# Expert stage of a two-layer inference step: a sixth place for weights, loads in the order in which places come free, and two blocks in the loop

## What is computed

```python
g_idx = jnp.argmax(g_logits, axis=-1)                 # one of 4 groups
top_v, top_i = lax.top_k(e_sel, TOP_K_IN_GROUP)       # 2 of its 8 experts
...
for g in range(N_GROUPS):
    a = jnp.einsum('td,edf->tef', x, w_gate[g])       # 1024 -> 256
    u = jnp.einsum('td,edf->tef', x, w_up[g])
    hid = jax.nn.silu(a) * u * comb[:, g, :, None]
    y = y + jnp.einsum('tef,efd->td', hid, w_down[g]) # 256 -> 1024
```

## Time and profile before

| What | us |
|---|---|
| median of 3 runs (1677.84 to 1684.67) | 1681.57 |
| profiled execution, its own time | 1689.48 |
| its span, first to last instruction | 1687.8 |
| PE busy | 1295.8 (77%) |
| DVE busy | 642.0 (38%) |
| ACT busy | 429.5 (25%) |
| POOL busy | 253.2 (15%) |

### The profile page before, as it was taken

How to read it: one execution, slowest core, us unless ns; L and a number is a source line. 1 busy time by engine, 2 the same in 40 slices (tenths; PEclk the granted TensorE clock), 3 DMA queues, 4 the chain that set the end, 5 groups by cost and what they waited for, 6 DMA issues and landing times. The chain is left out here.

```text
span 1687.8 us, 24274 instructions
## 1 busy us (share of the span) xinstructions
PE 1295.8 (77%) x8176; PEld 904.7 (54%) x8176; DVE 642.0 (38%) x1579; ACT 429.5 (25%) x971; POOL 253.2 (15%) x376
## 2 busy tenths in 40 slices
PE   6888899988838888777178898899797397787650
PEld 4777778867635444333145676667586253444320
DVE  4555544335452222212632343344463422222118
ACT  3555544443011101001111243344510111100010
POOL 0111122210111121221310000000011112211214
PEclk9988889998958988988588999999898599888775
DMA  4212224305077999983710000000031899999733
GB/s 152 65 58 65 78 90 151 107 15 197 38 305 266 394 395 385 393 285 125 277 42 16 14 28 14 14 13 14 30 125 41 328 370 392 377 386 359 278 102 108
DMA packets 59634, 290.91 MB, mean 172 GB/s; under 512 B 12209, under 2 KB 22641, under 8 KB 42497
## 3 DMA queue, kind: packets, MB, share of 16 engines
q1 hardware_dynamic: 49280, 270.62, 42.8%
q0 software_dynamic: 10240, 18.90, 3.7%
HBM read 274.86 MB, written 29.29 MB: 180 GB/s over the span
## 5 line engine op out<-in xcount | busy, mean ns | idle before, releaser
L1741 PE MATMUL psum<-w_gu,moe_experts_xgT 128*64 128x256 f32 x2048 | 264.1, 403 | 25.1 <-DVE moe_experts_xgT L1804 21.3
L1741 PEld LDWEIGHTS psum<-w_gu,moe_experts_xgT 128*64 128x64 f32 x2048 | 152.7, 147 | 138.5 <-issue 84.3
L1789 ACT ACTIVATE moe_experts_yo<-psum 64x512 f32<-64x512 f32 x64 | 37.8, 590 | 396.5 <-DMA y_d<-moe_experts_yo,moe_slots 333.4
L1816 DVE COPY moe_experts_yo<-psum 64x512 f32<-64x512 f32 x64 | 44.3, 693 | 242.1 <-DMA y_d<-moe_experts_yo,moe_slots 200.2
L1757 PE MATMUL psum<-w_dn,moe_experts_hidT 128*64 128x512 f32 x416 | 126.0, 736 | 9.6 <-issue 9.6
L194 PE MATMUL psum<-x_hi,ab_w_hi 128*128 128x288 f32 x384 | 126.7, 330 | 4.3 <-DVE ab_k_tok L852 3.2
L1731 PE MATMUL psum<-ident,mix 64*128 64x64 f32 x512 | 48.6, 241 | 98.4 <-DMA mix<-x_d,moe_tokens 98.3
L195 PE MATMUL psum<-x_lo,ab_w_hi 128*128 128x288 f32 x384 | 116.8, 304 | 0.0
L196 PE MATMUL psum<-x_hi,ab_w_lo 128*128 128x288 f32 x384 | 116.7, 304 | 0.0
L1804 DVE COPY moe_experts_xgT<-psum 128x512 f32<-128x512 f32 x64 | 44.3, 692 | 177.1 <-PE psum L1731 177.0
L1731 PEld LDWEIGHTS psum<-ident,mix 64*128 64x128 f32 x512 | 40.4, 151 | 126.4 <-issue 126.4
(11 more groups left out here) (289 smaller groups left out, 2297.8 us busy)
## 6 DMA issues: line engine op xcount, KB each, us to landing
w_gu<-in_w_gate_up SPq DMA_DIRECT2D x64, 2048.0 KB, 20.4
w_dn<-in_w_down SPq DMA_DIRECT2D x52, 1024.0 KB, 14.8
xT<-in_w_down SPq DMA_DIRECT2D x12, 1024.0 KB, 15.6
w_gu<-in_w_out SPq DMA_DIRECT2D x4, 2048.0 KB, 17.1
w_gu<-y_d SPq DMA_DIRECT2D x16, 512.0 KB, 7.1
xT<-cum_d SPq DMA_DIRECT2D x8, 544.0 KB, 7.2
w_q<-in_w_ab SPq DMA_DIRECT2D x8, 512.0 KB, 7.4
w_k<-in_w_ab SPq DMA_DIRECT2D x8, 512.0 KB, 8.2
```

The costliest lines, as they stand in the source:

```text
L1741: last = nc.tensor.matmul(gu(s)[h * CB:(h + 1) * CB, 0:EH], xgT[:, s % 2, j, :], w_gu[n][:, j, h * EH:(h + 1) * EH], start=(j == 0), stop= ...
L1816: nc.vector.tensor_copy(yo[s % 2][:, BANK:D], y(s)[CB:P, :]).then_inc(y_dve, 1)
```

## The change

- `DEEP` is 6. The down tiles of places 4 and 5 and a quarter of the gate/up tile of place 5 lie in `xT`; that gate/up tile is loaded by two DMAs (12 KB and 4 KB per partition). Six experts are loaded ahead of the expert stage.
- SP issues gate/up of b+1 ahead of down of b, in the order up(b+1-6), down(b-6) in which PE is done with them.
- The loop has `TRIP` = 2 blocks (30 and 31 here); 0 to 29 are written out. Each written-out run and each trip is now a chain of its own: PE and DVE end the last block's work ahead of the next chain's first block.
- POOL alternates gather and scatter in the loop.
- g and b are loaded at the end of SP's list, into place 2, and no longer have tiles of their own.
- In place of common counters each place has its own count of uses; `copy_x` and `copy_h` lose a second wait.

```diff
-DEEP = 5
-FIRST = NE - RING
+DEEP = 6
+TRIP = 2
+FIRST = NE - TRIP
@@ route, SyncE
-                prefetch_down(k, sp, layer, [0, 1])
                 for n in range(2, DEEP):
+                    prefetch_down(k, sp, layer, [n - 2])
                     prefetch_gate_up(k, sp, layer, [n])
-                    prefetch_down(k, sp, layer, [n])
+                prefetch_down(k, sp, layer, [DEEP - 2, DEEP - 1])
@@ experts
-            for b in range(FIRST):
-                step(b, b % RING, 0, b + 1 < FIRST)
+            def chain(blocks):
+                first(*blocks[0])
+                for n, block in enumerate(blocks):
+                    step(block, blocks[n - 1] if n else None, blocks[n + 1] if n + 1 < len(blocks) else None)
+                last(*blocks[-1])
+            chain([(b, b % TRIP, 0) for b in range(FIRST)])
             with eng.Fori(0, n_trips) as i:
-                first_of_trip(RING * i + FIRST, 0, i)
-                for s in range(RING):
-                    step(RING * i + FIRST + s, s, i, s + 1 < RING)
-            last(RING * n_trips + FIRST - 1, RING - 1)
+                chain([(TRIP * i + FIRST + s, s, i) for s in range(TRIP)])
@@ experts, SyncE
-                sp.dma_start(r["g"][:], k.ln_g[layer, 1:2, :].to_broadcast([P, D])).then_inc(r["g_in"], 16)
-                sp.dma_start(r["b"][:], k.ln_b[layer, 1:2, :].to_broadcast([P, D])).then_inc(r["g_in"], 16)
                 for b in range(DEEP, FIRST):
                     n = b % DEEP
-                    sp.wait_ge(gu_ready, b - DEEP + 1)
-                    load_gate_up(k, sp, layer, b, gu_in[n], w_gu[n])
-                    sp.wait_ge(y_ready, b - DEEP + 1)
-                    load_down(k, sp, layer, b, dn_in[n], w_dn[n])
+                    sp.wait_ge(gu_used[n], b // DEEP)
+                    load_gate_up(k, sp, layer, b, gu_in[n], k.w_gu[n])
+                    if b > DEEP:
+                        n = (b - 1) % DEEP
+                        sp.wait_ge(dn_used[n], (b - 1) // DEEP)
+                        load_down(k, sp, layer, b - 1, dn_in[n], w_dn[n])
...
+                sp.wait_ge(gu_used[2], len(range(2, FIRST, DEEP)))
+                sp.dma_start(r["g"], k.ln_g[layer, 1:2, :].to_broadcast([P, D])).then_inc(r["g_in"], 16)
+                sp.dma_start(r["b"], k.ln_b[layer, 1:2, :].to_broadcast([P, D])).then_inc(r["g_in"], 16)
@@ experts, GpSimd
                 with pool.Fori(0, n_trips) as i:
-                    for s in range(RING):
-                        gather(RING * i + FIRST + s, s, RING * i + s + 1)
-                    for s in range(RING):
-                        scatter(RING * i + FIRST - RING + s, s, RING * i + s + 1)
+                    for s in range(TRIP):
+                        gather(TRIP * i + FIRST + s, s, i, TRIP * i + s + 1)
+                        scatter(TRIP * i + FIRST - RING + s, s, TRIP * i + s + 1)
@@ experts, VectorE
-                    hold(dve, passed, (x_turned, b + 1), *since(gu_ready, b - 1))
+                    hold(dve, passed, done(x_used, b, s, trip, RING))
@@ mixer_out_and_mixture
-        k.w_dn = [c.enter_context(k.nc.sbuf_tensor(f"w_dn{n}_{layer}", [P, JE, D], F32))[:, :, :] for n in range(DEEP - 1)]
+        k.w_gu.append([c.enter_context(k.nc.sbuf_tensor(f"w_gu{DEEP - 1}_{layer}", [P, J - 2, 2 * EH], F32))[:, :, :],
+                       room[:, 2 * JE * D:2 * JE * D + 4 * EH].rearrange("p (j n) -> p j n", j=2)])
+        k.w_dn = [c.enter_context(k.nc.sbuf_tensor(f"w_dn{n}_{layer}", [P, JE, D], F32))[:, :, :] for n in range(DEEP - 2)]
+        k.w_dn += [room[:, n * JE * D:(n + 1) * JE * D].rearrange("p (j n) -> p j n", j=JE) for n in range(2)]
```

More of the change, by code:

```diff
@@ L1191, in mix_out @@
         lg = banks(k, 0, 1)
[L1193 removed]
+        w = [k.w_gu[h][0] for h in range(2)]
         w_hi = [sb(f"w_hi{h}", [P, J, BANK]) for h in range(2)]
@@ L1632, in place @@
+        def place(b, s, trip, ring):
             if isinstance(b, int):
[L1633 to L1641, removed]
+                return b % ring, b // ring + 1
+            return (FIRST + s) % ring, trip + (FIRST + s) // ring + 1
@@ L1772, in last, with step @@
-                def last(b, s):
-                    turn_hid(b, s)
-                    down(b, s, at_ring(s), n_trips + loads_before(at_ring(s)))
-                turn_x(0, 0, 0)
+                    last.then_inc(dn_used[n], 1)
+                def step(block, before, after):
+                    up(*block, 0)
+                    if before:
+                        turn_hid(*before)
+                    up(*block, 1)
+                    if after:
+                        turn_x(*after)
+                    if before:
+                        down(*before)
@@ L1814, in out @@
-                def out(b, s):
-                    hold(dve, passed, (y_ready, b + 1), *since(y_out, 16 * (b - 1)))
-                    nc.vector.tensor_copy(yo[s % 2][:, BANK:D], y(s)[CB:P, :]).then_inc(y_dve, 1)
-                def step(b, s, trip, ahead):
-                    first, before = isinstance(b, int) and b == 0, (s - 1) % RING
-                    if not first:
-                        copy_h(b - 1, before)
-                    if ahead:
-                        copy_x(b + 1, (s + 1) % RING)
-                    hidden(b, s)
-                    if not first:
-                        out(b - 1, before)
@@ L1833, in _, with step, last @@
+                def step(block, before, after):
+                    if before:
+                        copy_h(*before)
+                    if after:
+                        copy_x(*after)
+                    hidden(*block)
+                    if before:
+                        out(*before)
+                def last(b, s, trip):
+                    copy_h(b, s, trip)
+                    out(b, s, trip)
                 each_block(dve, n_trips, step, copy_x, last)
```

189 lines of the change are left out of this document (100 added, 89 removed).

## The result

| | before | after |
|---|---|---|
| median, us (runs) | 1680.27 (1677.84 to 1684.67) | 1657.36 (1656.31 to 1660.53, 4 runs) |
| profiled execution, its span | 1689.48, 1687.8 | 1656.31, 1654.5 |

The ratio is 0.9846 (95% interval 0.9813 to 0.9880): 1.5% faster, 22.9 us by the medians. The forecast was 12.7 us, 0.75%. The two profiled executions differ by 33.3 us; that of before lay 9.2 us above its median, so what follows reads single stretches in the traces and leaves the sum to the medians. By stretch, the 33.3 us are 3.5 ahead of the first scatter, 8.1 and 7.0 in the two expert stages, 11.7 between them and 2.9 behind the last scatter (59.1 against 56.2 us).

What follows compares the result with a forecast made beforehand. A chain of scatters was taken to bound the expert stages. Two stages at 7.5 us less, minus 2.3 for later starts, gave 12.7 us off the median 1681.57: 1669 us, range 1656 to 1683.

Steps and rivals of the forecast that it cites:

- What bounds the stage: Expert stage: a chain of scatters, each landing before the next, sets the pace at 9.25 us a block.
- when the loads end: First expert stage: the last down tile lands at 759 us, against 780.2 before.
- the end of the stage: First stage, without the start's shift: the last scatter lands at 794.9 instead of 802.4, 7.5 us less.
- The drain: Last blocks of the stage: up(30) waits for DVE's copy behind scatter 27 and starts at 774.0 us.
- The start: First gathers of both stages meet 7.3 us more of loads; block 0 starts 0.6 and 1.7 us later, 2.3 together.
- The rest: Moved g and b loads, use counts, dropped DVE waits and the split tile's extra issue: all hidden or nothing.
- C: Rival, start of the stages: the longer preload holds the first gather back, giving the gain back; 1677 us, chance 0.14.
- D: Rival, end of the stages: scatters 25 to 27 still meet full loads, a stage loses 5.4 us; 1695 us, chance 0.11.
- A: Rival, expert stages: loads end before scatter 24 is issued, about 5 us a stage more gain; 1659 us, chance 0.09.
- B: Rival, expert stages: weights set the pace, stage ends 767, 35 us less per stage; 1614 us, chance 0.04.

Runs made afterwards that it cites:

- e2: The kernel before with eight more short memsets on DVE at the start of latent attention, moving its loop; 1673.39 us, ratio 0.9932.
- e1: The changed kernel with six more short memsets on DVE at the start of latent attention, putting its loop back; 1672.14 us, ratio 0.9918.
- e6: The changed kernel with three more short memsets on DVE ahead of the loop of latent attention; 1659.12 us.
- e7: The changed kernel with nine more short memsets on DVE ahead of the loop of latent attention; 1666.56 us.
- e3: The changed kernel with one landing count per output buffer in place of one for all scatters; 1623.13 us, ratio 0.9645.
- e10: The changed kernel with the old order of issues from block 6 on, gate/up then down of the same block; 1665.61 us, ratio 0.9901.
- e5: The kernel before with one landing count per output buffer in place of one for all scatters; 1653.38 us, ratio 0.9827.

## Why the prediction was right, and where it failed

**The expert stages: right.** What bounds the stage, about when the loads end, and the end of the stage (7.5 us less; 8.1 and 7.0) came as worked out. e2 against the changed kernel is the change without the stops: (0.9932 - 0.9846) x 1681 = 14.5 us, uncertain by some 7, against 12.7. That the loads end at 758.7 where 759 stood is partly luck: this execution's stage began 3.5 us earlier, and counted from the first scatter they end after 235.3 and 233.9 us, where 759 - 526.94 = 232.1 was forecast. Inside, errors of some us cancelled too: scatter 24 came 740.87 - 523.44 = 217.4 us behind scatter 0, where 222.0 was forecast, since the first six blocks of that stage were faster (49.8 us against 54.9); in the second stage it took 226.4. Behind scatter 24 the first stage took 47.3 us and the second 39.3, where 43.4 was forecast. The drain was as described: up(30) waits for DVE's copy, 244.9 us behind scatter 0 where 247.1 stood. PE in time, the changed kernel:

```profile
768.30 5.36 PE L1760 MATMUL psum<-w_gu,moe_experts_xgT 128*64 128x256 f32 x32 [2.28 <-DVE moe_experts_xgT L1822]
```

**The start: right in its sum.** Gathers land 0.8 and 0.5 us later. Scatter 0 comes 1.6 and 0.6 us later behind the first gather's issue; 0.6 and 1.7 were forecast, so the sum, 2.2 against 2.3, fits by luck. e1, e6 and e7, with the same stage code, come 0.8 to 2.4 us later in sum.

**The rest: this step failed.** The paragraph "The rest" costed all else at nothing (the use counts and the two waits dropped on DVE: "nothing"), and the sum took in only the two stages and their start. The step asked of every removed wait and instruction what it costs where it stands; it didn't ask where the code behind it comes to stand. Six instructions fewer on DVE moved a later loop off a bad place. That is worth 12.1 us by e1 and 11.4 by e2; in the traces the stretch between the stages is 11.7 us shorter, through 5.5 us of PE's waits and some 7 of its lower clock. The rows were there: "issue" stops of 6.5 us at two jumps back are in the waits of before, 200 us behind the stage that I read. Forecast and missing term together, 12.7 + 12.1 = 24.8 us, stand against 22.9 by the medians and 25.9 by the ratio.

**The rivals.** C didn't come: the gathers landed in 8.4 and 7.0 us behind the longer preload. D didn't: scatters 26 and 27 were issued at 758.62 and 763.50, when the last weight tile had landed or was about to (758.7). A's time, 1659, is near the result, but its mechanism isn't there: the loads ended when forecast. B, weights as the pace, didn't come either, but e3 shows its mechanism and that it was priced too high: 35 us a stage were forecast, and e3's stages are 25.6 and 24.2 us shorter than before. The last scatter lands 7.3 + 2.6 = 9.9 us behind the last weight tile, near B's 8.0, but the weights end 240 us behind scatter 0 and not 232. That e3's 1623 lies near B's 1614 is luck: some 12 us of e3's gain come from the loop. My words "a chain of scatters sets the pace" were right of the wait and incomplete of the cause: the full DMA engines set both the landing of a scatter and the pace of the loads, and the two are 9.3 and 9.5 us by one cause. The change ends the loads 18 us earlier (235.3 us behind scatter 0, 253.3 before); scatters up to 24 keep their pace, so only the last ones gain by it, and the stage gets 7 to 8 us shorter.

**Open.** Why the old order of issues costs 4 us a stage with the chain (e10). Why the clock falls behind DVE's stops in the kernel before and in e1 and not in e5. The traces of single executions differ by some us in stretches that no edit touches, and no run here says why.

## What to carry to other kernels

When a change alters the number of instructions ahead of a loop, compare the rows "issue" at the loop's jumps back, and the instruction queue's packets, over the whole program: where they show a stop, some padding ahead of the loop is worth trying (8 memsets brought 11 us here). Then look at the engine that sets the pace, for what the stop really costs: its own waits, and its clock behind them. When a chain of waits and a full set of DMA engines show the same pace, look at how far the work lags its loads: taking the chain away brings the lag once and not a faster pace. And one count for all scatters made each wait here for the one before; a count per buffer brought 34 us.

## What the hardware showed that I had not expected

- At a jump back in its loop of 260 instructions DVE stood for 6.1 to 6.5 us at one place, 4.2 + 1.8 us one instruction ahead of it, and under 1 us two places ahead of that or three behind the first.
- Through two stops of 6.5 us on DVE, TensorE waited 5.5 us, and then ran for 13.6 us at a granted clock of 0.50; behind e5's, of 4.2 + 1.8 us, it stayed at 1.00.
- With a third less to load, a scatter still took 6.2 us to land, beside engines 95% busy at 332 GB/s; 3.0 us was the median behind the last weight loads.
- The same engines, full, moved 432 GB/s with weights alone (480 to 490 us, after) and 378 to 391 beside gathers and scatters.
